# The four adaptive modulations of a transformer block: from TensorE to GpSimd products and ScalarE row sums

## The reference, cut to what matters

```python
def adaln_params(c, w, b):                 # c [1, 1024], w [1024, 3072], b [3072]
    m = jax.nn.silu(c) @ w + b
    shift, scale, gate = jnp.split(m, 3, axis=-1)
    return shift[:, None, :], scale[:, None, :], gate[:, None, :]

def second_block(x, c, positions, ada_w, ada_b, ...):
    for i in range(DEPTH):                 # DEPTH = 2
        shift, scale, gate = adaln_params(c, ada_w[i, 0], ada_b[i, 0])
        h = x * (1.0 + scale) + shift
        ...                                # attention or retention: y
        x = layer_norm_2(ALPHA * x + (1.0 + gate) * y, ln_g[i, 0], ln_b[i, 0])
        shift, scale, gate = adaln_params(c, ada_w[i, 1], ada_b[i, 1])
        h = x * (1.0 + scale) + shift
        y = grouped_moe(h, ...)
        x = layer_norm_2(ALPHA * x + (1.0 + gate) * y, ln_g[i, 1], ln_b[i, 1])
    return x
```

```python
for layer in range(DEPTH):
    mix = even_mixer(h, ...) if layer % 2 == 0 else odd_mixer(h, ...)
    h = layer_norm(ALPHA * h + mix, ln_g[layer, 0], ln_b[layer, 0])
    h1 = causal_depthwise_conv(h @ w_up, conv_w) + conv_b    # 1024 -> 5632, 3 taps
    gate, val = jnp.split(h1, 2, axis=-1)
    ffn = (jax.nn.silu(gate) * val) @ w_down                 # 2816 -> 1024
    h = layer_norm(ALPHA * h + ffn, ln_g[layer, 1], ln_b[layer, 1])
```

## Time and profile before

| | us |
|---|---|
| median of three runs | 1744.45 (1744.38 to 1747.34) |
| profiled execution | 1745.01 |
| its span in the trace | 1743.3 |
| TensorE busy | 1621.2 (93%) |
| VectorE busy | 958.5 (55%) |
| ScalarE busy | 665.9 (38%) |
| GpSimd busy | 284.7 (16%) |

### The profile page before, as it was taken

The page is one execution under the profiler, slowest core; times in us unless marked ns, Lnnn a source line. Parts: engine busy times, 40 slices in busy tenths (PEclk is TensorE's granted clock), DMA queues, the critical chain, the costliest instruction groups (busy, mean ns, idle before and its releaser), DMA issues. The chain is left out here.

```text
span 1743.3 us, 26323 instructions
## 1 busy us (share of the span) xinstructions
PE 1621.2 (93%) x10612; PEld 1219.3 (70%) x10612; DVE 958.5 (55%) x1680; ACT 665.9 (38%) x1089; POOL 284.7 (16%) x241
## 2 busy tenths in 40 slices
PE   9999998999999989899999989997889999899976
PEld 9897874799887544899888864442379898643432
DVE  4576764788541574788564766121166957742112
ACT  3458212566431223566446442110143456411111
POOL 0354000163111120263101302000000300020000
PEclk9999999999999989899999999998999999999999
DMA  8432394555444584545424766999954665799996
GB/s 302 159 114 97 119 372 186 204 192 209 169 193 169 193 338 146 221 177 206 169 97 146 292 279 252 426 426 427 389 214 145 198 221 178 296 385 426 427 426 267
DMA packets 51634, 429.49 MB, mean 246 GB/s; under 512 B 5932, under 2 KB 6192, under 8 KB 9392
## 3 DMA queue, kind: packets, MB, share of 16 engines
q1 hardware_dynamic: 48528, 417.59, 61.2%
q0 software_dynamic: 2256, 7.88, 1.3%
q10 hardware_dynamic: 720, 2.23, 0.4%
HBM read 426.62 MB, written 1.05 MB: 245 GB/s over the span
## 5 line engine op out<-in xcount | busy, mean ns | idle before, releaser
L88 ACT ACTIVATE arena<-ps 128x384 f32<-128x384 f32 (+5 forms) x221 | 96.6, 437 | 458.5 <-PE ps L82 246.9
L82 PE MATMUL ps<-xsplit_f,wsplit_f 128*128 128x256 f32 x2112 | 255.7, 284 | 2.6 <-ACT xsplit_f L88 1.3
L82 PEld LDWEIGHTS ps<-xsplit_f,wsplit_f 128*128 128x128 f32 x2112 | 254.3, 192 | 4.2 <-ACT xsplit_f L88 2.1
L82 PE MATMUL ps<-ringx,arena 128*64 128x512 f32 (+1 forms) x1120 | 247.8, 612 | 7.9 <-DMA ringx<-in_md 5.1
L82 PE MATMUL ps<-ring,arena 128*32 128x512 f32 (+2 forms) x736 | 205.0, 613 | 33.6 <-DMA ringx<-in_mu 23.5
L91 DVE TENSOR_TENSOR wsplit_f<-ring,wsplit_f 128x1024 fp32r<-128x1024 f32 x132 | 180.6, 1372 | 80.8 <-ACT wsplit_f L88 80.8
L82 PEld LDWEIGHTS ps<-ring,arena 128*32 128x32 f32 (+2 forms) x736 | 68.7, 138 | 143.9 <-issue 131.9
L91 DVE TENSOR_TENSOR ringlo<-ring,ringhi 128x1024 fp32r<-128x1024 f32 x100 | 135.2, 1367 | 57.3 <-ACT ringhi L88 57.0
L88 ACT ACTIVATE wsplit_f<-ring 128x1024 fp32r<-128x1024 f32 x132 | 138.1, 1050 | 68.3 <-PE ps L82 56.6
L82 PEld LDWEIGHTS ps<-ringx,arena 128*64 128x64 f32 (+1 forms) x1120 | 73.3, 129 | 122.1 <-issue 116.7
L88 ACT ACTIVATE ringhi<-ring 128x1024 fp32r<-128x1024 f32 x124 | 129.3, 1052 | 72.5 <-PE ps L82 53.4
(11 more groups left out here) (215 smaller groups left out, 2645.4 us busy)
## 6 DMA issues: line engine op xcount, KB each, us to landing
ringx<-in_md SPq DMA_DIRECT2D x56, 1024.0 KB, 22.2
ring<-in_wu SPq DMA_DIRECT2D x22, 2048.0 KB, 7.8
ring<-in_ada SPq DMA_DIRECT2D x20, 2048.0 KB, 9.3
ringx<-in_mu SPq DMA_DIRECT2D x40, 1024.0 KB, 16.2
ringx<-in_mg SPq DMA_DIRECT2D x36, 1024.0 KB, 13.7
ring<-in_mg SPq DMA_DIRECT2D x28, 1024.0 KB, 18.4
ring<-in_mu SPq DMA_DIRECT2D x24, 1024.0 KB, 19.9
ring<-in_wd SPq DMA_DIRECT2D x10, 2048.0 KB, 7.7
```

What stands on the lines that cost most here:

```text
L82: return self.e.matmul(o, l, r, start=start, stop=stop, skip_group_check=True)
L88: return self.e.activation(o, i, f, **k)
```

## The change: what it does

The 24 pieces on TensorE go, with all that VectorE and the ring did for them. The weights are laid out anew, transposed, as 96 pieces of 128 outputs by 1024 inputs (512 KB each). `gate` now holds `c` in all 128 partitions (a broadcast DMA of the SP queue), over which ScalarE applies SiLU once. For each piece

- GpSimd multiplies it by that row, in place (`ada` on its lane: 128x1024),
- ScalarE copies it onto itself with `accum_out`, which leaves the sum of each row in one column of `mods`, and then issues the DMA of the piece that comes into this buffer next, on its own queue.

There are two buffers for pieces 0 to 5 (`tmpn` and one more) and five from then on. 32 pieces are made in the even stage, 19 in FFN 0, 26 in the odd stage, 19 in FFN 1. The biases and the layer-norm products that VectorE made as the pieces came are made by `modulations`, 20 small operations at the end of FFN 1. In the even stage ScalarE's table loads for SiLU and its activation of `c` move from behind the high halves to behind the fifth. `ELSEWHERE` and `FOURTH`, the places of the loads in the odd stage, go; these loads now take ring slots in turn.

The diff, cut to what acts on the device:

```diff
@@ SP queue, all_loads
-    out += [("ada", k // 6, k % 6) for k in range(12)] + [("woe", 0), ("woe", 1)]
+    out += [("woe", 0), ("woe", 1)]
...
-    ada = [("ada", 2 + k // 6, k % 6) for k in range(12)]
-    out += [("wo", 0), ("wo", 1), ("wo", 2), ada[0], ("wov", 0), ("wo", 3), ("wov", 1)] + ada[1:]
+    out += [("wo", 0), ("wo", 1), ("wo", 2), ("wov", 0), ("wo", 3), ("wov", 1)]
...
+        s.dma_start(gate[:, :], ins["c"].broadcast_to([128, 1024])).then_inc(s_c, 16)
@@ TensorE
-        def ada_piece(s, k):
...
-                    for c in range(4):
-                        r = mm(b[32 * c:32 * c + 32, :], scb[:, 2 * c + kk, :], view[:, 2 * c + kk, :], kk == 0, kk == 1)
...
-                        ada_piece(0, k - 6)
...
-                        ada_piece(1, j)
@@ VectorE
-        def ada_piece(s, k):
...
+        def modulations():
+
+            v.wait_ge(*a("ads", 95))
+            for i in range(4):
+                o = 24 * i
+                tt(mods[:, o:o + 8], mods[:, o:o + 8], C("adab", o, o + 8), ALU.add).then_inc(s_dve, v.did())
...
             for i in range(47, 66):
                 split(i)
+            if l:
+                modulations()
             norm(n, lambda i: ps("dn", n, i), False)
@@ ScalarE
+        def ada_load(k):
+            a.dma_start(pieces[ADA_BUF[k]], ins["ada"][k]).then_inc(s_ada[ADA_BUF[k]], 16)
+
+        def ada(k):
+
+            piece = pieces[ADA_BUF[k]]
+            a.wait_ge(*g("adm", k))
+            act(piece, piece, ACT.Copy, accum_out=mods[:, k:k + 1]).then_inc(s_act, a.did("ads", k))
+            if k in ADA_NEXT:
+                a.own()
+                ada_load(ADA_NEXT[k])
...
+                if n == 4:
+                    tables("silu_and_others")
+                    a.wait_ge(s_c, 16)
+                    act(gate[:, :], gate[:, :], ACT.Silu).then_inc(s_act, a.did("c"))
+                    tables("natural_log_exp_and_others")
+                    for k in range(2):
+                        ada_load(k)
+                if n in (9, 10):
+                    ada(n - 9)
...
+            ada(2)
+            ada(3)
             for i in range(12, 16):
                 high_half(0, i)
+            ada(4)
+            ada(5)
...
+                if k == 6:
+                    for i in (8, 9, 10):
+                        ada_load(i)
+                if k >= 6:
+                    ada(2 * k - 6)
+                    ada(2 * k - 5)
...
+                if i % 4 == 3 and j:
+                    ada(ADA_FFN[l] + j - 1)
...
             for i in range(49, 66):
                 high(i)
+                if i % 2:
+                    ada(ADA_FFN[l] + 10 + (i - 49) // 2)
...
             for n in (4, 5, 6, 7):
                 tile(n)
+                ada(ADA_ODD + n - 4)
...
             for n in (10, 11):
+                for k in range(4):
+                    ada(ADA_ODD + 4 * n - 36 + k)
                 tile(n)
...
+                    if k >= 5:
+                        ada(ADA_ODD + 7 + k)
@@ GpSimd
+        def ada(k):
+            piece, b = pieces[ADA_BUF[k]], ADA_BUF[k]
+            g.wait_ge(*a("c"))
+            g.wait_ge(s_ada[b], 16 * ADA_COUNT[k])
+            g.tensor_tensor(piece, piece, gate[:, :], ALU.mult).then_inc(s_pool, g.did("adm", k))
+
...
                 g.tensor_tensor(m.gsp[:, 1, gg, :], y, m.gsp[:, 0, gg, :].bitcast(F32), ALU.subtract) \
                     .then_inc(s_pool, g.did("gsp", n, gg))
+                if gg % 2 == 0:
+                    ada(ADA_FFN[l] + gg // 2)
+            for k in range(11, 19):
+                ada(ADA_FFN[l] + k)
             norm(n)
...
             rows_applied(2)
+            for k in range(12):
+                ada(ADA_ODD + k)
...
                     g.tensor_tensor(O.acc[th], O.acc[th], O.mt[th], ALU.add).then_inc(s_pool, g.did("gla", i, th))
+                for k in range(2):
+                    ada(ADA_ODD + 10 + 2 * i + k)
             norm(2)
...
+        ada(0)
+        ada(1)
         g.wait_ge(*v("hrow"))
...
         load_rows(0)
+        for k in range(2, 6):
+            ada(k)
...
+        for k in range(6, 32):
+            ada(k)
         norm(0)
```

More of the change, by code:

```diff
@@ L168, with ada_buffers @@
 ADA = 13
+ADA_FIRST = 6
+ADA_FFN = (32, 77)
+ADA_ODD = 51
+def ada_buffers():
+    buf, count, following, last, used = [], [], {}, {}, {}
+    for k in range(96):
+        b = k % 2 if k < ADA_FIRST else (k - ADA_FIRST) % 5
+        used[b] = used.get(b, 0) + 1
+        buf.append(b)
+        count.append(used[b])
+        if b in last:
+            following[last[b]] = k
+        last[b] = k
+    return buf, count, following
+ADA_BUF, ADA_COUNT, ADA_NEXT = ada_buffers()
 R8 = tuple(range(8))
@@ L295, in all_slots @@
         else:
-            if name in ELSEWHERE:
-                i = ELSEWHERE[name]
-            else:
-                i = turn % SLOTS
-                turn += 1
+            i = turn % SLOTS
+            turn += 1
         used[i] = used.get(i, 0) + 1
@@ L449, in emit @@
     s_rows = sem("second_rows_landed")
+    s_c, s_ada = sem("c_landed"), [sem(f"ada{i}_landed") for i in range(5)]
     s_par = sem("params_landed")
@@ L588, in emit @@
         m = Arena(st, 2, 25600)
-        O.ring = m.ap[:, 21504:25600]
         O.qc = rows(m.take(2048), 8, 256)
```

81 lines of the change are left out of this document (10 added, 71 removed).

## The result

| | before | after |
|---|---|---|
| median, us | 1744.85 | 1826.28 |
| profiled execution, us | 1745.01 | 1826.38 |
| its span | 1743.3 | 1824.7 |

A forecast was written before the change was run, and what follows sets the result against it. TensorE, busy 93% of the span, was taken as the bound, the other engines following closely. FFNs 48, even stage 2, odd stage 8 and FFN 1's end 1.4 made +59.4 on 1745.0, less 0.56: about 1804 us, range 1750 to 1830.

The forecast's parts named there:

- two slow rivals: Ports taken in turn (1830 us, chance 0.08) and TensorE going cold (1829 us, chance 0.10).
- The FFN rounds: FFN up products: rounds of 15.2 us with a row operation, 12.8 plain, against TensorE's 11.52; 22.6 us per FFN.
- The down products: Start of FFN down products: eight GpSimd pieces in a row, +1 to +3 us together with the stall put off.
- The even stage: +3 us (0 to +6) ahead of the delta rule's levels, 0 in them; 2 counted for the stage.
- The levels of the delta rule: Even stage: 24 products from about 209 to 277-282 us, levels 12 us or more with masks, under 10 later; net 0.
- The odd stage: Gated attention: levels of 11.7 us instead of 9.9 (+4), 6 to 8 at the end; +8 taken (-4 to +16).
- What goes: TensorE's 24 pieces, 45 us, and the wait for the output product's weights, 3.75 us: 1696 if nothing else changed.
- The end of FFN 1: 20 small VectorE operations, 4.2 us, behind the last sum, delaying the first residual: +1.4 us.
- the faster one: TensorE's time comes back if ScalarE waits under 1.7 us per FFN round and delta-rule levels shorten: 1710 us, chance 0.14.
- The cover in the FFNs: GpSimd's product finds the port free and ends before ScalarE asks; FFNs cost 5 us each at most: 1766, chance 0.15.
- The ports in turn: Each mask, low half and softmax step behind its own GpSimd product: even +12, odd +14, FFNs +30 each; 1830, chance 0.08.
- The cold clock: TensorE's clock drops after waits in some 18 long rounds and 8 levels, 20 to 30 us more: 1829, chance 0.10.

The follow-up runs named there:

- e4: Changed kernel with the FFN's modulation product behind the low half of the odd gate product instead of the even one: 1801.9 us.
- e3: Changed kernel without the first eight of GpSimd's 96 products, their sums taking plain weights: 1821.1 us.
- e6: Kernel before, with c as a tensor of its own in HBM instead of eight columns of the parameter tensor: 1752.8 us, ratio 1.0040.
- e11: Kernel before, with the parameter tensor eight columns narrower and c as a tensor behind all others: 1753.8 us, ratio 1.0044.
- e12: Kernel before, with the parameter tensor eight columns narrower in HBM, c behind all tensors, but its SBUF tile padded to the old width: 1746.1 us, ratio 1.0003.
- e1: Changed kernel without GpSimd's 96 products, ScalarE summing plain weights: 1877.4 us with other routing; 876.4 up to the last residual of FFN 1.
- e5: Changed kernel without any piece (no fetch, product or sum): 1711.9 us in all, 855.7 up to the last residual of FFN 1.

## Why the prediction was right, and where it was short

The 22 us between 59.4 and 81.4 are 7.9 in the even stage (+9.9 for the +2 counted), 7.4 in the two FFNs and their end, and 6.7 in the second block; the odd stage came out as summed. So the direction and the costliest mechanism were foreseen, and the range held since its upper bound came from two slow rivals that were not the reason.

- **The FFN rounds: right in mechanism and size.** 15.2 and 12.8 us forecast, 15.21 and 12.85 measured, and e4 shows that the place in GpSimd's order is it. A sum with its issue held ScalarE for 1.57 us there (479.65 to 481.22), not 1.75. The stage was put at 24 us and was 27.2 and 29.6. The four long and six plain rounds give 4 x 3.7 + 6 x 1.3 = 22.6 as forecast, of which 18.4 had come by the first down product.
- **The down products: mis-sized.** With what the chunks ahead put off they were to add 1 to 3 us to the 22.6, and FFN 0 came to 4.6 over it. The low halves at 3.35 us are near the 3.6 of the working; the wait of 3.53 us ahead of them and the colder clock behind it (0.66; 3.3 us more for 72 products) were not in the sum.
- **The even stage: the step that failed.** +3 ahead of the levels was forecast, 11.6 measured; e3 puts 9.05 on the first eight products. The prediction looked at the low halves and the softmax for the shared ports and passed over VectorE's steps on 12 columns, which take 0.2 us alone and 2 beside GpSimd, and over the masks at 183 us. Products 6 and 7 stand nowhere in its working, which has six ahead of the levels and 24 in them, of 32; GpSimd made them at 182.57, beside those masks. The rest goes with the narrower parameter tensor (e6, e11, e12).
- **The levels of the delta rule: near the forecast by luck.** The products were to run from 209 on and end at 277 to 282; they began at 225.76, since piece 8 was fetched late, and ended at 283.5. The levels were to take 12 us or more with masks and under 10 later, and a level of 9 was named as a sign of being wrong: they took 11.5, 8.0 and 20.2. From the first mask product to the last round of additions (199.34 to 253.93, and 210.97 to 267.26) it is 54.6 and 56.3 us, +1.7, and the tail gave back 3.4, near the 0 taken.
- **The odd stage: right in sum, by errors that cancel.** Level 3 came 1.6 us earlier (about 3 forecast), a level was put at 11.7 and measured at 13.0, which makes +12.4, and from the last level on, where 6 to 8 us were to come on top, the stage got back 2.9: +7.9 for +8. The prediction's own terms, +4 and 6 to 8, add up to 10 to 12, and it took 8. e1 and e5 show that the products did all of it.
- **What goes.** 45 + 4 us were taken for TensorE's pieces; 42.6 came back in e5, with 2.3 lost again in FFN 1. The even stage gave more than its twelve pieces and the wait (29.1 for 22.8 + 3.75), the odd one less (15.8 for 22.8); TensorE had been waiting for 12 of 95 us there already. That the pieces had filled part of such waits is argued, not shown.
- **The end of FFN 1.** +1.4 forecast; FFN 1 lost 2.4 more than FFN 0, and 2.3 in e5 without any piece.
- **The second block.** 0 forecast, +6.7 measured, a step that the prediction did not have at all: a parameter tile 32 bytes narrower.

Of the rivals, the faster one failed on its condition: ScalarE waited 2.6 us for the odd gate product in plain rounds, more than the 1.7 at which it would have cost nothing. That TensorE's time can come back e1 shows (876.4 against 898.4), but without GpSimd's products. The cover in the FFNs did not hold. The ports in turn were seen in the last two groups of masks (4.50 and 8.67 for 2.55 us), in the masks at 183 us and in the low halves of the down products. That rival's sum, +86, lies nearer to the 81.4 than the forecast's 59, and its +30 for an FFN nearer to 27.2 and 29.6 than 24; but the rounds kept the forecast's lengths and its +12 and +14 for the even and the odd stage were 9.9 and 7.9, so the nearness of the total shows little. The cold clock came in FFN 0 behind the one wait of 3.53 us, about as long as the 3.75 named in the prediction, and not in the long rounds; in the gated attention (0.77 for 0.93) and the delta rule (0.87 for 1.00) it was lower too, and what that cost was not measured.

**Left open:** where the rest of the 10.1 us of slower products in an FFN comes from; why the levels begin 1.4 to 2.4 us later with the narrower parameter tensor, in one trace each (e6, e11, e12), and whether that is in the time of e12 at all, which is that of before; what makes the second block vary between 850.9 and 854.8 us among the kernels with the narrow tile; and by what rule the SBUF address acts on the DMA (one shift, 32 bytes, was tried).

## What to carry to other kernels

Work that moves from the fullest engine to an idle one is paid where it stands in that engine's order and in what its operations hold up: here the 43 us saved (e5) cost 117 (973.0 less 855.7). Look for the smallest steps of the other engine beside it, since a step of 0.2 us pays the same wait as one of 1.2. A fused product and sum on the engine that already has the ports was worth more than two idle engines, but only in the stages where that engine had room.

## What the runs showed of the hardware that was not expected

- A DMA's rate depended on the address of its SBUF destination: 427 GB/s with the tiles at one place (e12), 420 with those behind the parameters 32 bytes lower (e11), the same HBM layout in both; the second block took 6 to 8 us more.
- VectorE operations on 12 columns of SBUF took 1.80 to 2.27 us beside GpSimd operations on SBUF, a `tensor_scalar` (2.13) as much as a `tensor_tensor`. The Trainium skill (SBUF — State Buffer, "SBUF: two separate sides") has the pair of ports locked for a whole instruction, for operations of VectorE in a two-port mode or, beside a GpSimd operation that reads SBUF, with two SBUF inputs. The rows agree: the step begun at 69.08, just behind a product, ended at 71.21, when that product (68.84 to 71.18) was done. In which mode the `tensor_scalar` ran no row shows.
- scalar_tensor_tensor with accum_out over 128x1024 took 1.22 us and 0.08 for the accumulator, no more than the plain product of two tiles (1.22).
